# Dilated attention's groups in the order of dilations 4, 16, 1, and a new order of work on ScalarE and VectorE

## The chip, the core and the metric

One NeuronCore of a Trainium2 chip runs the whole program. The metric is device time in microseconds of one execution, the median of several runs. The engines are TensorE (matmuls), VectorE, ScalarE, GpSimd and SyncE; each works through its own queue in order and waits on semaphores for the others.

## What is computed

Two transformer blocks follow each other, on 1024 tokens of width 1024. The first has a convolution layer and a layer of dilated attention, the second has neighbourhood attention, retention and an MLP. The change touches dilated attention alone:

```python
DILATION_GROUPS = ((128, 1), (512, 4), (2048, 16))   # (window, dilation)

def dilated_attention_branch(h, cos, sin, w_in, q_norm, k_norm, w_out):
    q, k, v, gate = jnp.split(h @ w_in, ...)          # 3 groups x 8 heads x 64, gate 512
    q = partial_rope(rms_norm(q, q_norm), cos, sin)
    k = partial_rope(rms_norm(k, k_norm), cos, sin)
    for g, (window, dilation) in enumerate(DILATION_GROUPS):
        o, lse = dilated_band_attention(q[:, :, g], k[:, :, g], v[:, :, g], dilation, window // dilation)
    wts = softmax(stack(lses), axis=0)                # over the three groups
    o = sum(wts[..., None] * stack(outs), axis=0)
    return (o * silu(gate)) @ w_out
```

Each group splits the tokens by residue modulo the dilation; within a residue a query sees itself and up to 128 earlier keys of its own residue. The three outputs of a head are weighted by a softmax over the groups' log denominators.

## The kernel before

Activations stay in SBUF with features on partitions. A matmul with weights ("linear") multiplies a 1024x128 weight tile with all 1024 tokens, in three steps of split precision (high part with high part, high with low, low with high) and two halves of 512 columns: 8 k-tiles of 6 matmuls, 48 in all, into one of two PSUM buffers A and B. SyncE loads weight tiles in pairs in the order of their use, GpSimd splits each into a high and a low part (w_hi, w_lo).

Attention works on four pairs of heads. A pair has ten linears: q, k and v of three groups and the gate. `pair` runs three times in a loop and once more with `last`. Its order is written out by hand on each engine:

- **A group** (`dilated`) has 8 units of 128 queries. In unit u TensorE does the six matmuls of one k-tile of some linear (`products`, L516), the scores of unit u (L723), the product with V of unit u-2 (`values`, L699) and the transposes of the probabilities of unit u-1 (`turn`, L613). VectorE masks the scores and takes the negated maximum (L1745), ScalarE takes the exponential and its sum (`probabilities`, L1202) and later copies the turned probabilities to SBUF as pt (`copy_turned`, L1212), and VectorE takes out the output (`take_out`, L1757). The scores of unit u+1 wait for VectorE's pass over unit u, the product with V for ScalarE's copy.
- A unit has one or two key blocks of 128 (`attn_keys`): dilation 1 has two in each unit but the first, dilation 4 in every other one, dilation 16 one. Units with two have twice the columns in every step.
- The products with V of units 6 and 7 stand inside the next linear, at k = 3 and k = 5 (`rest`).
- **Between groups**, q and k of the next group are prepared: VectorE evacuates the linear (L1591), ScalarE squares it and applies the gain (`square_and_gain`, L1171, L1172), four DMAs issued by ScalarE exchange the rotary halves (`swap_parts`, L1180), VectorE rotates (`rope`, L1774 to L1777), TensorE sums the squares of each head (L536), ScalarE makes inverse roots of them (`roots`), and VectorE applies them while it sorts the tokens by residue (`normalise`, L1783, L1785; `values_in` for v, L1812). For dilation 1 no sorting is needed.
- In dilations 4 and 16 a unit's rows are not the tokens in their order, so the maxima and sums of these groups (`st_own`) go to DRAM by DMA and come back in the tokens' order (`load_stats`, L1241, into `st_x`). Dilation 1 writes `st_x` directly.
- **The shares**: VectorE takes the least of the three negated maxima (`shifts`, L1819), ScalarE exponentiates, VectorE divides (`shares`), ScalarE widens each share to 64 columns (`widen`, L1249), TensorE turns it (`turn_share`, L613), and VectorE multiplies it into the group's output O (`weigh`, L1838). The widened tiles use the buffers wide0, q_sq and vT.
- **The last pair** has no linear under its third group. Behind it come the shares of this pair, the rounding of the four y tiles into high and low parts (`round_ys` on ScalarE, L1307; `split_ys` on VectorE, L1900), and the output projection, whose first two parts cover the first three tiles and then wait for the fourth.

## Time and profile before

| | us |
|---|---|
| median of 3 runs | 2728.7 (2721.8 to 2732.0) |
| profiled execution, its own time | 2727.0 |
| its span in the trace | 2725.2 |
| TensorE busy | 2535.5 (93%) |
| the attention stage | about 640 to 1330 |
| one linear inside it, from 913.3 to 924.3 | 11.0 |

The profile shows one execution. "Busy" counts instructions on an engine, "idle before" the time in front of one with what ended it, PEclk is the clock granted to TensorE as a share of full speed. Lines L... are lines of the kernel.

### The profile page before, as it was taken

To read this page: it belongs to the slowest core of one execution; us is meant where nothing else is said; L and a number is where in the kernel's file an instruction comes from. 1 tells how busy PE (TensorE), PEld (TensorE's weight loads), DVE (VectorE), ACT (ScalarE), POOL (GpSimd) and SP (SyncE) were. 2 spreads that over 40 slices of the span, in tenths; PEclk is the share of its full clock that TensorE was granted. 3 is DMA by queue.
4 is the path that set the end of the run, shared out by engine and by line. 5 is a ranking of instruction groups with operands and counts; after the bars stand their busy time and mean duration, and the time that the engine had idled before them with its cause. 6 is when DMAs were issued, how large, how long until landed. Compare 5 with 4: busy or idle time off the path is not lost.

```text
span 2725.2 us, 31511 instructions
## 1 busy us (share of the span) xinstructions
PE 2535.5 (93%) x11924; PEld 1961.4 (72%) x11924; DVE 1239.4 (45%) x1673; ACT 847.0 (31%) x1263; POOL 866.2 (32%) x437
## 2 busy tenths in 40 slices
PE   7999669999999999898799999999999999999996
PEld 5877348676666666676577677787788888888884
DVE  6999853444544443554644555544421121111223
ACT  5555442324444443444332323322221010010111
POOL 2888743221221221312122222222233333333332
PEclk9999879999999999998899999999999999999998
DMA  3111202111111111111011211221111111111111
GB/s 122 47 46 46 85 11 70 39 53 39 36 36 35 36 28 39 37 36 36 21 59 44 52 41 42 72 66 35 39 46 47 54 47 47 48 53 46 46 46 69
DMA packets 70876, 129.48 MB, mean 48 GB/s; under 512 B 37880, under 2 KB 40952, under 8 KB 70776
## 3 DMA queue, kind: packets, MB, share of 16 engines
q1 hardware_dynamic: 30096, 107.27, 12.5%
q10 hardware_dynamic: 40680, 20.76, 3.4%
q8 instruction: 76, 1.25, 0.2%
q14 instruction: 24, 0.20, 0.0%
HBM read 117.39 MB, written 4.33 MB: 45 GB/s over the span
## 4 chain that ended last, share of the span: by engine, by line
PE 70%; DVE 12%; issue 6%; ACT 5%; ACTq 2%; DMA 2%; POOL 1%; DVEq 0%; SPq 0%; POOLq 0%
PE ps_A L516 31%; PE ps_B L516 26%; PE ps_B L590 2%; PE ps_C L613 2%; PE ps_D L613 2%; POOL ta L451 1%; PE ps_B L723 1%; ACTq L1180 1%; PE ps_C L699 1%; DVE ssum L1564 1%; PE ps_D L699 1%; DMA qT<-q_in 1%; PE ps_A L723 1%; DVE ps_C L1610 1%; DVE kT L1785 1%
## 5 line engine op out<-in xcount | busy, mean ns | idle before, releaser
L433 POOL CAST w_hi<-w_raw 128x1024 fp32r<-128x1024 f32 x162 | 180.3, 1113 | 1686.2 <-issue 805.3
L426 POOL TENSOR_TENSOR w_lo<-w_raw,w_hi 128x1024 fp32r<-128x1024 f32 x188 | 472.0, 2510 | 61.0 <-ACT w_hi L1025 48.0
L516 PE MATMUL ps_A<-HA_hi,w_hi 128*128 128x512 f32 x960 | 313.8, 408 | 48.3 <-POOL HA_lo L475 22.6
L516 PE MATMUL ps_A<-HA_lo,w_hi 128*128 128x512 f32 x960 | 299.3, 393 | 0.0
L516 PE MATMUL ps_A<-HA_hi,w_lo 128*128 128x512 f32 x960 | 299.1, 393 | 0.0
L516 PE MATMUL ps_B<-HA_hi,w_hi 128*128 128x512 f32 x832 | 267.2, 403 | 3.5 <-DVE G L1591 3.3
L516 PE MATMUL ps_B<-HA_lo,w_hi 128*128 128x512 f32 x832 | 258.5, 392 | 0.0
L516 PE MATMUL ps_B<-HA_hi,w_lo 128*128 128x512 f32 x832 | 257.3, 390 | 0.0
L516 PEld LDWEIGHTS ps_A<-HA_hi,w_hi 128*128 128x128 f32 x960 | 176.0, 190 | 97.7 <-issue 47.3
L516 PEld LDWEIGHTS ps_A<-HA_lo,w_hi 128*128 128x128 f32 x960 | 182.2, 190 | 39.2
L516 PEld LDWEIGHTS ps_A<-HA_hi,w_lo 128*128 128x128 f32 x960 | 182.1, 190 | 39.2
L516 PE MATMUL ps_A<-HB_hi,w_hi 128*128 128x512 f32 x640 | 204.0, 400 | 6.8 <-DVE HB_lo L2031 4.2
L1505 ACT ACTIVATE sq<-ta 128x1024 f32<-128x1024 f32 x32 | 34.0, 1062 | 529.7 <-DVE ta L2163 529.7
L516 PE MATMUL ps_A<-HB_lo,w_hi 128*128 128x512 f32 x640 | 198.3, 391 | 0.0
L516 PE MATMUL ps_A<-HB_hi,w_lo 128*128 128x512 f32 x640 | 198.0, 391 | 0.0
L516 PEld LDWEIGHTS ps_B<-HA_lo,w_hi 128*128 128x128 f32 x832 | 157.6, 189 | 33.7
L516 PEld LDWEIGHTS ps_B<-HA_hi,w_lo 128*128 128x128 f32 x832 | 157.0, 189 | 33.6
L516 PEld LDWEIGHTS ps_B<-HA_hi,w_hi 128*128 128x128 f32 x832 | 153.2, 190 | 37.7 <-issue 8.7
L516 PE MATMUL ps_B<-HB_hi,w_hi 128*128 128x512 f32 x512 | 161.1, 396 | 0.0
L516 PE MATMUL ps_B<-HB_lo,w_hi 128*128 128x512 f32 x512 | 157.8, 389 | 0.0
L516 PE MATMUL ps_B<-HB_hi,w_lo 128*128 128x512 f32 x512 | 157.6, 389 | 0.0
L516 PEld LDWEIGHTS ps_A<-HB_hi,w_hi 128*128 128x128 f32 x640 | 118.6, 189 | 35.1 <-issue 8.0
(335 smaller groups left out, 3805.4 us busy)
## 6 DMA issues: line engine op xcount, KB each, us to landing
w_raw<-w_dram SPq DMA_DIRECT2D x188, 512.0 KB, 3.5
X<-x_dram SPq DMA_DIRECT2D x8, 512.0 KB, 8.6
X<-x_dram ACTq DMA_DIRECT2D x8, 512.0 KB, 7.2
out_dram<-X SPq DMA_DIRECT2D x8, 512.0 KB, 2.8
wp_sb<-wp_dram ACTq DMA_DIRECT2D x16, 128.0 KB, 2.0
qT<-q_in ACTq DMA_DIRECT2D x48, 32.0 KB
kT<-k_in ACTq DMA_DIRECT2D x48, 32.0 KB
p_A<-p_dram ACTq DMA_DIRECT2D x2, 512.0 KB, 4.2
```

The source lines that it names most:

```text
L426: pool.tensor_tensor(w_lo[q][:, :, :], w_raw[q][:, :, :], w_hi[q][:, :, :].bitcast(F32), ALU.subtract).then_inc(S[f"w_ready{q}"], 1)
L433: pool.tensor_copy(w_hi[q][:, :, :], w_raw[q][:, :, :]).then_inc(S["w_rounded"], 1)
L451: pool.tensor_tensor(accp[u][:, :], (tap_out[0] if j == 0 else accp[u])[:, :], tap_out[(j + 1) % 2][:, :], ALU.add).then_inc(S["pool_tap"], 1)
L516: op = pe.matmul(AB[b][:, cols], wt[:, w0 + k, :], act[:, k, cols], start=(first and k == ks[0] and step == 0), stop=(last and k == ks[-1] ...
L590: op = pe.matmul(AB[b][:, cols], wp_sb[t][:, k, :], p_sb[k][:, cols], start=(k == 0), stop=(k == PLE_K - 1))
L613: op = pe.transpose(CD[b][:, c * P:(c + 1) * P], src(c), ident[:, :])
L699: op = pe.matmul(CD[slots[u]][d, T - P:T], V[:, k0 + c, d], pt[u % 2][:, (h * nk + c) * P:(h * nk + c + 1) * P], start=(c == 0), stop=(c = ...
L723: op = pe.matmul(AB[other][:, at:at + nk * P], qT[rows, u * P:(u + 1) * P], kT[rows, k0 * P:(k0 + nk) * P], start=True, stop=True)
L1180: act.dma_start(dst[at + d:at + d + ROT_HALF, :], src[at + e:at + e + ROT_HALF, :]) \
L1505: act.activation(sq[:, :], ta[:, :], ACT.Square).then_inc(S["u_sq"], 1)
L1564: dve.tensor_tensor(ssum[:, :], ssum[:, :], sq[:, :], ALU.add).then_inc(S["ssum_added"], 1)
L1610: op = dve.scalar_tensor_tensor(out, win, tap, acc, ALU.mult, ALU.add)
```

## The change

The groups run in the order of dilations 4, 16, 1 (indices 1, 2, 0); the weight tiles are loaded in the matching order. Both exchanges of statistics are then issued before the third group, and the third group needs none. Besides:

- ScalarE's Square of the next q moves from behind unit 1 to behind unit 3, its gain to behind unit 5. The swap of q is issued before k's Square and before the copy of unit 7, the swap of k behind that copy.
- VectorE rotates q before it takes out unit 7 and rotates k before `values_in`.
- TensorE turns the second share at k = 4 and the third at k = 6 of the linear (before: at k = 0 and k = 4). In the last pair it turns two shares before the output projection's first part and the third behind it.
- In the last pair the rounding of the first three y tiles moves into the third group (units 2, 4, 6), and VectorE makes their low parts behind `shares`.

```diff
 N_VEC = _at
+ORDER = (1, 2, 0)
+QKV = [3 * g + k for g in ORDER for k in range(3)] + [9]
+
+
 NA_BLOCKS = [(cb, half) for cb in range(4) for half in range(2)]
 NA_BAND = (0, 8, 24, 32)
 NA_SORT = (2, 1, 1, 0)
...
             sp.dma_start(head_ones[:, :], mats[2]).then_inc(S["head_ones_loaded"], 16)
             sp.dma_start(perm[:, :], mats[3]).then_inc(S["perm_loaded"], 16)
-            with n.loop(sp, ATTN_AT // 2 + 1, w_ready0=1, w_ready1=1) as i:
+            with n.loop(sp, ATTN_AT // 2 - 1, w_ready0=1, w_ready1=1) as i:
                 weight_pair(i * 2 + 2, i * 2 + 3)
+            weight_pair(ATTN_AT + QKV[0], ATTN_AT + QKV[1])
+            weight_pair(ATTN_AT + QKV[2], ATTN_AT + QKV[3])
             with n.loop(sp, PAIRS - 1, w_ready0=5, w_ready1=5) as j:
                 t = j * 10 + ATTN_AT
                 for a, b in ((4, 5), (6, 7), (8, 10), (9, 11), (12, 13)):
-                    weight_pair(t + a, t + b)
-            at = ATTN_AT + 10 * (PAIRS - 1) + 4
+                    weight_pair(*(t + c // 10 * 10 + QKV[c % 10] for c in (a, b)))
+            at = ATTN_AT + 10 * (PAIRS - 1)
+            for c in (4, 6, 8):
+                weight_pair(at + QKV[c], at + QKV[c + 1])
+            at += 10
             with n.loop(sp, (RET_AT - at) // 2, w_ready0=1, w_ready1=1) as i:
                 weight_pair(i * 2 + at, i * 2 + at + 1)
...
                 def shares(k):
                     if k == 0:
                         turn_share(0)
+                    if k == 4:
                         turn_share(1)
-                    if k == 4:
+                    if k == 6:
                         turn_share(0)
-                rest = dilated(0, 0)
+                rest = dilated(ORDER[0], 0)
                 linear(1, HA, pre=sums_at(6, rest))
                 linear(0, HA)
-                rest = dilated(1, 1)
+                rest = dilated(ORDER[1], 1)
                 linear(0, HA, pre=sums_at(6, rest))
                 linear(1, HA)
                 if last:
-                    rest = dilated(2, None)
+                    rest = dilated(ORDER[2], None)
                     rest(3)
                     rest(5)
                     return
-                rest = dilated(2, 0)
+                rest = dilated(ORDER[2], 0)
                 linear(1, HA, pre=rest)
                 linear(0, HA, pre=sums_at(4))
                 linear(1, HA, pre=shares)
...
             pe.wait_ge(S["w_ready0"], n.next("w_ready0"))
             b0 = take_ab()
+            turn_share(0)
+            turn_share(1)
             out_part(b0, 0, 0, range(PAIRS - 1))
-            for i in range(GROUPS):
-                turn_share(i)
+            turn_share(2)
             b1 = take_ab()
             out_part(b1, 0, 1, range(PAIRS - 1))
             out_part(b0, 0, 0, [PAIRS - 1]).then_inc(S["half_done"], 1)
...
                 act.activation(cosT[:, :], turn_of[:, :], ACT.Sin, scale=0.5).then_inc(S["half_sin"], 1)
                 act.activation(sinT[:, :], turn_of[:, :], ACT.Sin).then_inc(S["sin_ready"], 1)
-            def square_and_gain(name, src, sq_of):
-
-                after_ab()
+            def square(name, src, sq_of):
+
                 act.activation(sq_of[:, :], src[:, :], ACT.Square).then_inc(S[name + "_sq"], 1)
+
+            def gain(name, src):
+
                 act.activation(src[:, :], src[:, :], ACT.Identity, scale=col(name + "_gain")) \
                     .then_inc(S[name + "_gained"], 1)
+
+            def square_and_gain(name, src, sq_of):
+
+                after_ab()
+                square(name, src, sq_of)
+                gain(name, src)
             def swap_parts(name, src, dst):
...
                     act.wait_ge(S[f"cd_free{b}"], n.now(f"cd_free{b}"))
                     act.activation(root[:, :], root[:, :], ACT.Exp, scale=-0.5).then_inc(S[name + "_root_ready"], 1)
-            def dilated(g, queries):
+            def dilated(g, queries, between=lambda u: None):
                 def probabilities(u):
                     nk = attn_keys(g, u)[1]
...
                 b, free = next_cd()
                 act.copy(V[:, :, :].rearrange("p b d -> p (b d)"), CD[b][:, :]).then_inc(free, 1)
                 probabilities(1)
-                if queries:
-                    square_and_gain("q", q_in, q_sq)
                 for u in range(2, BLOCKS):
                     copy_turned(u - 2)
                     probabilities(u)
+                    if queries and u == 3:
+                        after_ab()
+                        square("q", q_in, q_sq)
+                    if queries and u == 5:
+                        gain("q", q_in)
+                    between(u)
                 copy_turned(6)
                 def rest():
-                    copy_turned(7)
                     after("unit_done")
                     after("unit_done")
                     act.wait_ge(S["probs_ready"], n.next("probs_ready", BLOCKS))
...
                         for src, dst in stats_moves(st_own[:, g - 1], g, g):
                             act.dma_start(dst, src).then_inc(S["stats_stored"], 16)
                             n.next("stats_stored", 16)
-                return rest
+                return copy_turned, rest
             def load_stats(g):
...
                 settle()
                 act.activation(y_at[:, j, :], y_at[:, j, :], ACT.Silu).then_inc(S["gate_silu"], 1)
+            def round_ys(k):
+                act.copy(YS[0][:, k, :], y_at[:, k, :]).then_inc(S["ys_hi"], 1)
+
+            def early_ys(u):
+
+                if u == 2:
+                    act.wait_ge(S["y_done"], PAIRS - 1)
+                if u in (2, 4, 6):
+                    round_ys(u // 2 - 1)
+
             def pair(j, last):
                 for g in range(2):
-                    rest = dilated(g, True)
+                    copy_turned, rest = dilated(ORDER[g], True)
+                    swap_parts("q", q_in, qT)
                     square_and_gain("k", k_in, k_sq)
+                    copy_turned(7)
+                    swap_parts("k", k_in, kT)
                     rest()
-                    swap_parts("q", q_in, qT)
-                    swap_parts("k", k_in, kT)
                     roots()
                     if g == 1:
-                        load_stats(1)
+                        load_stats(ORDER[0])
+                        load_stats(ORDER[1])
                     pass_ab()
                 if last:
                     after_ab()
                     silu_gate(j)
-                rest = dilated(2, not last)
+                copy_turned, rest = dilated(ORDER[2], not last, early_ys if last else lambda u: None)
+                if not last:
+                    swap_parts("q", q_in, qT)
+                copy_turned(7)
                 rest()
-                load_stats(2)
                 if last:
                     return
                 pass_ab()
-                swap_parts("q", q_in, qT)
                 exp_shares()
                 square_and_gain("k", k_in, k_sq)
                 swap_parts("k", k_in, kT)
...
                 pair(j, last=False)
             pair(PAIRS - 1, last=True)
-            def round_ys(k):
-                act.copy(YS[0][:, k, :], y_at[:, k, :]).then_inc(S["ys_hi"], 1)
-
-            act.wait_ge(S["y_done"], PAIRS - 1)
-            for k in range(PAIRS - 1):
-                round_ys(k)
             exp_shares()
             after("shared_ready")
             for g in range(GROUPS):
...
                         take_out(u - 2)
                 def rest():
-                    take_out(6)
-                    take_out(7)
                     after("turned", 2)
-                return rest
+                return take_out, rest
             def rope(name, src, dst):
...
             def pair(j, last):
                 for g in range(2):
-                    rest = dilated(g)
+                    take_out, rest = dilated(ORDER[g])
                     evacuate(k_in[:, :], g)
+                    take_out(6)
+                    rope("q", q_in, qT)
+                    take_out(7)
                     rest()
-                    rope("q", q_in, qT)
-                    values_in(g ^ 1, g + 1)
                     rope("k", k_in, kT)
-                    normalise(g + 1)
+                    values_in(g ^ 1, ORDER[g + 1])
+                    normalise(ORDER[g + 1])
                     if last and g == 1:
                         evacuate(y_at[:, j, :], 1)
                     else:
                         evacuate(q_in[:, :], g)
-                rest = dilated(2, not last)
+                take_out, rest = dilated(ORDER[2], not last)
                 if not last:
                     evacuate(y_at[:, j, :], 0)
+                take_out(6)
+                if not last:
+                    rope("q", q_in, qT)
+                take_out(7)
                 rest()
                 if last:
                     return
                 shifts()
                 evacuate(k_in[:, :], 1)
                 shares()
-                rope("q", q_in, qT)
                 rope("k", k_in, kT)
-                values_in(0, 0)
-                normalise(0)
+                values_in(0, ORDER[0])
+                normalise(ORDER[0])
                 for g in range(GROUPS):
                     weigh(g)
                 evacuate(q_in[:, :], 1)
...
             rotary_tables()
             rope("q", q_in, qT)
             rope("k", k_in, kT)
-            values_in(0, 0)
-            normalise(0)
+            values_in(0, ORDER[0])
+            normalise(ORDER[0])
             evacuate(q_in[:, :], 1)
             with n.loop(dve, PAIRS - 1, ab_free0=5, ab_free1=5, cd_free0=18, cd_free1=18, lin_done0=5, lin_done1=5,
                         q_swapped=192, k_swapped=192, q_root_ready=3, k_root_ready=3, dve_step=27, scores_done=24,
...
                 dve.tensor_tensor(YS[1][:, k, :], y_at[:, k, :], YS[0][:, k, :].bitcast(F32),
                                   ALU.subtract).then_inc(S["ys_ready"], 1)
+            shifts()
+            shares()
             for k in range(PAIRS - 1):
                 split_ys(k)
-            shifts()
-            shares()
             for g in range(GROUPS):
                 weigh(g)
             gated(PAIRS - 1)
```

## Rows read from the trace of the kernel before

**Rows 1.** The page, part 1: busy time of each engine

```profile
PE 2535.5 (93%) x11924; PEld 1961.4 (72%) x11924; DVE 1239.4 (45%) x1673; ACT 847.0 (31%) x1263; POOL 866.2 (32%) x437
```

**Rows 2.** Waits of TensorE, 640 to 1330 us: total, times, longest

```profile
PE ps_C L699 <- ACT pt L1212: 14.2, 9, 2.0
PE ps_A L516 <- DVE YS_lo L1900: 10.7, 2, 7.2
PE ps_D L613 <- ACT q_sq L1249: 9.8, 3, 3.3
PE ps_D L699 <- ACT pt L1212: 9.2, 5, 2.2
PE ps_B L723 <- DVE q_in L1591: 6.4, 3, 3.0
...
PE ps_A L723 <- DVE q_in L1591: 2.0, 4, 0.6
PE ps_A L723 <- DVE kT L1785: 1.9, 1, 1.9
```

**Rows 3.** Timeline, units of dilation 1: start, us, instruction

```profile
834.71 0.66 PE L699 MATMUL ps_D<-pt,V 128*64 128x128 f32 x8
...
836.82 0.56 ACT L1212 COPY pt<-ps_C 128x512 f32<-128x512 f32 x1
...
837.89 0.66 PE L699 MATMUL ps_C<-pt,V 128*64 128x128 f32 x8
```

**Rows 4.** Timeline, third unit of dilation 1

```profile
822.97 1.04 ACT L1171 ACTIVATE q_sq<-q_in 128x1024 f32<-128x1024 f32 x1
...
823.92 1.13 ACT L1172 ACTIVATE q_in<-q_in,vec 128x1024 f32<-128x1024 f32 x1
...
825.36 0.44 PE L699 MATMUL ps_C<-pt,V 128*64 128x128 f32 x4 [2.01 <-ACT pt L1212]
```

**Rows 5.** Timeline, units of dilation 4 (892), then of dilation 16

```profile
892.02 0.35 ACT L1212 COPY pt<-ps_D 128x256 f32<-128x256 f32 x1
...
892.68 0.44 PE L699 MATMUL ps_D<-pt,V 128*64 128x128 f32 x4
...
939.65 0.44 PE L699 MATMUL ps_C<-pt,V 128*64 128x128 f32 x4
...
941.28 0.35 ACT L1212 COPY pt<-ps_D 128x256 f32<-128x256 f32 x1
...
942.19 0.44 PE L699 MATMUL ps_D<-pt,V 128*64 128x128 f32 x4
```

**Rows 6.** A wait for a share; windows (seventh column PEclk) without and after a stall

```profile
801.55 0.69 PE L613 MATMUL ps_D<-ident,q_sq 128*128 128x128 f32 x2 [3.27 <-ACT q_sq L1249]
...
806.00:807.00 1.00, 1.00 (x6) 0.84 (x5) 0.96 (x2) 0.12 (x1) 0.00 (x0) 1.00 0.00 0
...
882.00:883.00 1.00, 1.00 (x4) 0.81 (x3) 0.00 (x0) 0.00 (x0) 0.00 (x0) 0.50 0.00 0
```

**Rows 7.** Timeline, swap of q and the rotation that waits for it

```profile
851.27 2.65 ACTq L1180 DMA_DIRECT2D qT<-q_in  x4
...
855.65 1.23 DVE L1774 TENSOR_TENSOR q_in<-q_in,cosT 128x1024 f32<-128x1024 f32 x1 [4.21 <-DMA qT<-q_in]
```

**Rows 8.** The last pair's third group: window, and a product with V

```profile
1288.00:1298.00 10.00, 10.00 (x51) 5.44 (x50) 4.42 (x26) 5.49 (x24) 0.00 (x0) 0.50 0.01 2
...
1288.86 0.69 PE L699 MATMUL ps_D<-pt,V 128*64 128x128 f32 x4
```

**Rows 9.** Last product with V, first matmul on the last rounded tile

```profile
1300.47 0.69 PE L699 MATMUL ps_D<-pt,V 128*64 128x128 f32 x4 [0.46 <-ACT pt L1212]
...
1325.88 0.73 PE L516 MATMUL ps_A<-YS_hi,w_hi 128*128 128x512 f32 x2 [3.43 <-DVE YS_lo L1900]
```

**Rows 10.** Timeline, statistics first used, share widened

```profile
1310.42 0.21 DVE L1819 TENSOR_REDUCE least<-st_x 128x16 f32<-128x48 f32 x1
...
1312.20 1.04 ACT L1249 COPY wide<-shared 128x1024 f32<-128x1024 f32 x1 [1.05 <-DVE shared L1830]
```

6 lines of the change are left out of this document (3 added, 3 removed).

## Prediction

> **What bounds the kernel now.** I read the page's engine shares first: TensorE is busy 93% of the span [rows 1], so time is only won where TensorE stands still or works at its lower clock. The change touches the attention stage alone, some 690 us from 640 to 1330 us, so the second view is TensorE's waits in that window [rows 2]. They sum to about 58 us, of four kinds: for ScalarE's copy of turned probabilities (pt), 14.2 + 9.2 us; for ScalarE's widened share, 9.8 us; for VectorE's evacuation of q_in (6.4 + 2.0 us) or its kT (1.9 us); and for the rounded y at the end (10.7 us). The timeline then says what each waits behind. Last, the granted clock: an ordinary microsecond shows 1.00 and six matmul records; one after a stall shows 0.50 and four [rows 6]. Those are the levels 2.4 and 1.2 GHz, so a stall costs more than its own length when the clock falls after it.
>
> **A. The square and gain of q leave the third unit.** In all 11 groups that load a next q, ScalarE runs Square and then gain (L1171, L1172) ahead of the first copy of probabilities, and TensorE waits 2.01 us [rows 4]. The Square takes 0.95 us from start to start; the gain is the rest, 1.04 us. The two pt rows of [rows 2] hold 23.4 us; 1.6 us belong to the last, bare group, so this edit is about 21.8 us. The operations are not removed but moved behind units 3 and 5, one at a time, where they delay the copy that the next unit needs. The slack there is the start of the product with V minus the end of the copy: dilation 1, 837.89 - 837.38 = 0.51 us [rows 3]; dilation 4, 892.68 - 892.37 = 0.31 us; dilation 16, 942.19 - 941.63 = 0.56 us [rows 5]. So each group keeps stalls of (0.95 - slack) + (1.04 - slack): 1.0, 1.4 and 0.9 us. Times 3, 4 and 4 groups that is 12.2 us; dilation 4's copy is still a little late in the third unit, 4 x 0.2, so 13 us stay and 8.8 us go. In three of the four dilation 4 groups the stall also pulled the clock to 0.50 for about 3 us [rows 6]; half of the work of those 3 us is lost, 1.5 us each, 4.5 us. Stalls of 0.7 us should not do that (the group that begins at 640 us stalled 2.0 us without a fall). **A = 13.3 us.** Bounds: no slack at all keeps 22 us and gives 4 us; full slack gives 26.
>
> **B. The second and third share are turned later.** TensorE turned two shares at k = 0 and waited 3.27 us for the second [rows 6], in each of three pairs: 9.8 us. Now it works through four k first, some 5.5 us, so the wait goes. Two of the three stalls were followed by half clock, again some 1.5 us each. VectorE weighs each output behind its turn; its chain gets the strided forms of dilation 4 at this place and ends about when the linear does, so I give it nothing and bound it with 1 us each. **B = 12.8 us** (9 to 14.5).
>
> **C. The chain between two groups.** The swap of q was issued behind the last copy and store, and VectorE idled for it [rows 7]; then it rotated q, took v, rotated k, normalised both and evacuated q_in, and TensorE's scores waited for that. Now the swap of q goes out before copy 7 and the rotation runs before the last output is taken; the swap of k follows, and its rotation runs ahead of values_in. Six operations of 1.23 us [rows 7], 7.4 us, leave the stretch before the scores, which is more than each single wait (0.5 to 3.0 us). What remains is that q_in can only be evacuated after its linear. Of 6.4 + 2.0 + 1.9 us [rows 2] I leave 0.05 us in each of 8 places. **C = 9.9 us** (6 to 10.3). ScalarE's four swap issues hold its queue 2.65 us [rows 7], now ahead of k's Square, k's gain and copy 7. Counted on from the end of copy 6 at 843.7 us, copy 7 ends at 849.2; TensorE asks for it at 850.5. Hidden with 1.3 us to spare.
>
> **D. The last pair.** Its third group runs with no linear under it. It was dilation 16 and becomes dilation 1. Under a linear the two differ by 3.18 - 2.54 = 0.64 us a unit at full clock [rows 3, 5]; the first units are alike, so the covered part wins 7 x 0.64 = 4.5 us. Bare, dilation 16 took (1300.47 - 1288.86) / 6 = 1.94 us a unit at clock 0.50 with TensorE's records full [rows 8]; dilation 1 adds twice 0.64: 3.22 us, and 7 units cost 9.0 us. The three roundings now inside this group (1.04 us each) push ScalarE past its slack by 0.2 us each: 0.6 us. The tail: from the last product with V to the last rounded tile was 1325.88 - 1300.47 = 25.4 us [rows 9], in it 9.2 us from the store at 1301.25 to the first use of the statistics at 1310.42 [rows 10], which goes. But TensorE now turns two shares before its 18 hidden matmuls, and the third turn stands behind these. New tail: last product and copy 1.7; statistics to widened share 1.8 [rows 10]; widen 1.1; two turns at half clock 3.3; 18 matmuls 5.0 (1.5 us of it at half clock); third turn 0.8; weigh and add 2.5, gate 1.2, round 1.1, low part 1.2; handovers 0.4. Sum 20.1 us: 5.3 us won. **D = 4.5 - 9.0 - 0.6 + 5.3 = +0.2 us.**
>
> The Trainium skill, TensorE: Matmul & The Clock Gate (Part 4: PE-mode transpose), says that transposes do not count as TensorE activity the way matmuls do. By that rule the two turns that now lead the tail would not help to raise the clock and the 18 matmuls behind them would run slow throughout, 6.6 us instead of 5.0, a loss of 1.6 us that moves no chance here; the rows of before hold no turns alone after an idle stretch in the tail, so they cannot say.
>
> The exchange of statistics itself, the change's namesake, is worth nothing in the first three pairs: VectorE waited for it, but no wait of TensorE hangs on it [rows 2]. The order of the weight tiles, their number and size stay as they were: zero.
>
> **Sum.** 13.3 + 12.8 + 9.9 + 0.2 = 36.2 us, against the profiled execution's 2727.0 us (span 2725.2): 2690.8 us. The median of before lies 1.7 us above that execution, so I forecast 2692 us, 1.3% faster. A measurement of this kernel tells about 0.5%, 13.6 us, from no change.
>
> **The rivals.**
> 1. *The stall of A is only moved.* If the moved Square and gain find no slack, because units run faster once the first stall is gone, A gives 4 us: 2702 us. For it: the slacks of 0.3 to 0.6 us are smaller than either operation. Against: the units after the stall already run at their steady length [rows 3]. Chance 0.16.
> 2. *The clock stays up in the bare group.* Dilation 1 gives TensorE twice the columns. At 1.00 its own work there is 1.6 us and the round through VectorE and ScalarE about 2 us, so 7 units cost 1 us less than now instead of 9 more, 2684 us with an allowance for the idle start. Against: 0.50 in all ten microseconds from 1288 [rows 8]. Chance 0.12.
> 3. *It does not do what it says.* The waits reappear one step on (A gives 4, B 5, C 3, D 0): 12 us, 2716 us, within 0.5%. For it: in-order queues on four engines often return a wait. Against: each freed wait has another engine's idle time behind it. Chance 0.07.
> 4. *Slower.* VectorE now rotates q before it takes output 7, and that frees the PSUM bank in which TensorE sums k's squares. If the swap lands late, TensorE stands at those sums. From [rows 7] a swap lands 4.4 us after its issue starts: 848.1, rotation to 851.8, output taken by 852.3; the bank is wanted at 854.3, 2 us to spare. The place occurs 8 times; to cost the 36 us won and 14 more, the output must be taken 6.3 us beyond that margin each time, over 8 us late. That gives 2742 us. Chance 0.04, for no swap in before landed so late.
>
> **Numbers.** My forecast has 0.61. The range must hold rivals 1 and 2, the bounds of A (4 to 26), B, C and D (-5 to +9): gains of 17 to 53 us, 2676 to 2712. Faster by over 0.5%: 0.61 + 0.16 + 0.12 = 0.89; within 0.5%: 0.07; slower 0.04.
>
> **What would show it.** The wait for pt at the third unit near zero, and two waits of 0.4 to 0.7 us at the fifth and seventh in each group with a linear (A). No wait for the widened share, and that linear 13.4 us long with its three turns (B). Waits for q_in at the scores under 0.1 us (C). About 3.2 us a unit at clock 0.50 in the bare group, and 20 us from the last product with V to the last rounded tile (D). I am wrong if the fifth and seventh units stall by 1 us or more, if the bare group keeps its clock, or if TensorE starts to wait at the head sums.

## The result

The changed kernel takes 2685.6 us (median of 4, 2685.5 to 2687.4) where the kernel before takes 2728.3 (2721.8 to 2732.0): a ratio of 0.9847, 95% interval 0.9828 to 0.9867. That is inside the range and 6 us below the forecast of 2692. The profiled execution's span is 2683.8 us, 41.4 less than before. First the page, then TensorE's waits in the same stage (total, times, longest); they answer to [rows 1] and [rows 2]:

```profile
PE 2525.6 (94%) x11924; PEld 1953.8 (73%) x11924; DVE 1249.2 (47%) x1673; ACT 849.0 (32%) x1263; POOL 852.5 (32%) x437
```

```profile
PE ps_C L708 <- ACT pt L1231: 9.1, 17, 0.8
PE ps_D L708 <- ACT pt L1231: 6.3, 12, 1.5
PE ps_B L732 <- DVE st_own L1774: 3.6, 3, 1.4
PE ps_C L622 <- ACT wide L1271: 3.4, 1, 3.4
PE ps_C L622 <- ACT sc L1221: 2.9, 4, 2.2
PE ps_A L525 <- DVE YS_lo L1932: 2.2, 1, 2.2
...
PE ps_A L732 <- DVE q_in L1620: 0.5, 1, 0.5
PE ps_B L732 <- DVE q_in L1620: 0.5, 1, 0.5
```

The reader should see four things. The waits for pt fell from 23.4 to 15.4 us, but in 29 pieces instead of 14. The waits for the share q_sq in three pairs are gone; behind the last pair's third group one of 3.4 us for `wide` and one of 2.2 us for the rounded y stand where 10.7 us stood for the rounded y. The waits for q_in and kT at the scores are nearly gone, 1.0 us of 10.3. And there is a wait that hardly was there before (0.2 us): the scores for VectorE's masking pass (st_own), 3.6 us in 3 pieces.

To place gains, all kernels below are measured by **the stage**: from the first scores of the first group to the first matmul on the last rounded tile. In the changed kernel those are these two rows of the timeline:

```profile
642.72 0.49 PE L732 MATMUL ps_B<-kT,qT 64*128 64x128 f32 x4
...
1291.90 0.73 PE L525 MATMUL ps_A<-YS_hi,w_hi 128*128 128x512 f32 x2 [2.21 <-DVE YS_lo L1932]
```

So its stage is 1291.90 - 642.72 = 649.2 us; before it was 1325.88 [rows 9] - 641.22 = 684.7 us. The stage won 35.5 us, the forecast's sum was 36.2. The other 5.9 us of the 41.4 lie in code that is the same in both kernels (below).

From the rows of the scores, one stretch after the other (us). A group is from its first scores to its eighth, a gap from there to the next group's first. A group is covered when TensorE has a linear under it. The bare group, the last pair's third, has none and is taken from its first scores to its last product with V; the tail runs from there to the end of the stage:

| | before | changed |
|---|---|---|
| pair 1, 2, 3: three groups with their gaps | 176.2, 177.5, 177.5 | 167.1, 168.9, 168.5 |
| group of dilation 1, covered | 23.0 | 22.2 |
| group of dilation 4, covered | 21.8 in pair 1, then 23.2 to 23.4 | 21.3 in pair 1, then 22.8, 22.6, 21.9 |
| group of dilation 16, covered | 19.5 | 18.7 |
| the three gaps of a pair, summed | 111.9, 111.6, 111.6 | 105.0, 105.1, 105.0 |
| last pair: two covered groups and gaps | 108.0 | 99.0 |
| last pair: bare group | 20.0 | 26.0 |
| last pair: tail | 25.4 | 19.8 |

### The profile page after: what moved, and what is told of

Its sections match the earlier page's. It is cut to its first block, busy times and chain, and to the rows that moved or that the text cites. A ratio compares the mean times of both kernels' runs of the same rounds, so it can differ in the third digit from the quotient of the medians.

```text
span 2683.8 us, 31485 instructions
## 1 busy us (share of the span) xinstructions
PE 2525.6 (94%) x11924; PEld 1953.8 (73%) x11924; DVE 1249.2 (47%) x1673; ACT 849.0 (32%) x1263; POOL 852.5 (32%) x437
## 4 chain that ended last, share of the span: by engine, by line
PE 74%; DVE 10%; issue 6%; ACT 5%; POOL 2%; ACTq 1%; DVEq 0%; DMA 0%; SPq 0%; POOLq 0%
PE ps_A L525 34%; PE ps_B L525 27%; PE ps_B L599 2%; POOL ta L460 2%; PE ps_C L622 1%; PE ps_D L622 1%; PE ps_C L545 1%; PE ps_D L545 1%; PE ps_B L732 1%; ACT sc L1221 1%; DVE ssum L1593 1%; DVE ps_C L1639 1%; PE ps_B L545 1%; DVE sc L1774 1%; PE ps_C L708 1%
## 5 line engine op out<-in xcount | busy, mean ns | idle before, releaser
L442 POOL CAST w_hi<-w_raw 128x1024 fp32r<-128x1024 f32 x162 | 171.3, 1058 | 1657.8 <-PE ps_A L525 794.5
L525 PE MATMUL ps_A<-HA_hi,w_hi 128*128 128x512 f32 x960 | 314.7, 409 | 46.7 <-POOL HA_lo L484 21.1
```

The lines of the kernel that those rows point to most:

```text
L442: pool.tensor_copy(w_hi[q][:, :, :], w_raw[q][:, :, :]).then_inc(S["w_rounded"], 1)
L525: op = pe.matmul(AB[b][:, cols], wt[:, w0 + k, :], act[:, k, cols], start=(first and k == ks[0] and step == 0), stop=(last and k == ks[-1] ...
```

## The experiments

Stage and rest of the span come from each kernel's own profile; the ratio is to the kernel before on the same chip. The changed kernel's stage came out the same in two profiles, the kernel before's 3.9 us apart, and the others have one profile each. So a difference of under 4 us in the stage (e2, e4, e7) is no proof by itself; what is said of these rests on the waits and gaps in their traces.

| kernel | median | ratio, 95% interval | stage | rest |
|---|---|---|---|---|
| changed | 2685.6 | 0.9847 (0.9828 to 0.9867) | 649.2 | 2034.6 |
| e1 Square back | 2709.1 | 0.9907 (0.9885 to 0.9929) | 667.4 | 2039.9 |
| e2 shares back | 2686.2 | 0.9831 (0.9811 to 0.9851) | 648.3 | 2030.4 |
| e3 chain back | 2692.4 | 0.9859 (0.9835 to 0.9883) | 655.5 | 2034.0 |
| e4 order back | 2690.2 | 0.9837 (0.9816 to 0.9859) | 651.8 | 2036.7 |
| e5 order and shares back | 2708.4 | 0.9922 (0.9895 to 0.9948) | 669.0 | 2038.0 |
| e6 halves | 2680.4 | 0.9815 (0.9790 to 0.9841) | 641.8 | 2037.7 |
| e7 SiLU late | 2686.6 | 0.9835 (0.9808 to 0.9862) | 647.0 | 2040.9 |
| e8 q normalised first | 2682.4 | 0.9826 (0.9800 to 0.9851) | 643.1 | 2031.9 |
| f9 before again | 2725.2 | 0.9994 (0.9976 to 1.0012) | 688.6 | 2032.8 |
| f10 Square alone | 2711.3 | 0.9941 (0.9919 to 0.9962) | 674.7 | 2039.8 |
| f11 changed again | 2687.8 | 0.9852 (0.9832 to 0.9872) | 649.2 | 2038.5 |
| f12 three additions | 2672.1 | 0.9804 (0.9784 to 0.9823) | 635.4 | 2043.3 |

### e1: Square and gain back behind unit 1

```diff
                 probabilities(1)
+                if queries:
+                    square_and_gain("q", q_in, q_sq)
                 for u in range(2, BLOCKS):
...
-                    if queries and u == 3:
-                        after_ab()
-                        square("q", q_in, q_sq)
-                    if queries and u == 5:
-                        gain("q", q_in)
```

> The changed kernel with q's Square and gain back behind unit 1. Measure: the stage, from the first scores of the first group to the first matmul on the last rounded tile (before 684.7 us, changed 649.2 us). Theory: the changed kernel still waits 10.9 us for pt in its 11 covered groups where the kernel before waited 21.8 us, and three of those stalls let the clock fall, so the stage grows by 11 to 15 us, with waits of about 2 us in each third unit and none in the fifth and seventh. Rival (the stall is only moved): under 5 us. Second rival (the clock is what counts): the stage grows by 4 us in the groups where the clock falls and nowhere else.

Measured: the stage grew by 18.2 us, more than the 11 to 15 expected. The waits for pt came back as single ones of 1.6 to 2.2 us at each third unit. The surplus is the clock: it fell behind seven of these eleven waits and not behind four, where the changed kernel has no fall under its covered groups. Dilation 1 lost it in all three pairs, and its group takes 24.6 us (23.0 in the first profile of the kernel before). That this comes from its new place is not shown: in the second profile of the kernel before (f9) dilation 1 lost it too, as the first group. The windows of that stall in pair 1 (seventh column: the granted clock):

```profile
749.00:751.00 2.00, 1.08 (x6) 0.32 (x5) 0.68 (x3) 2.00 (x6) 0.00 (x0) 1.00 0.14 57
751.00:753.00 2.00, 0.91 (x6) 0.61 (x7) 0.39 (x3) 2.00 (x6) 0.00 (x0) 0.81 0.00 0
753.00:756.00 3.00, 3.00 (x11) 2.17 (x10) 0.00 (x0) 0.62 (x2) 0.00 (x0) 0.55 0.00 0
```

Both rivals fell: 18.2 is far from 5, and groups that kept the clock grew too (dilation 16 in the first three pairs from 18.7 to 19.6).

### e2, e4, e5: the places of the shares and the order of the groups

```diff
                 def shares(k):            # e2, e5
                     if k == 0:
                         turn_share(0)
-                    if k == 4:
                         turn_share(1)
-                    if k == 6:
+                    if k == 4:
                         turn_share(0)
```

```diff
-ORDER = (1, 2, 0)                         # e4, e5
+ORDER = (0, 1, 2)
...
                     if g == 1:
-                        load_stats(ORDER[0])
-                        load_stats(ORDER[1])
+                        load_stats(1)
...
                 rest()
+                load_stats(2)
                 if last:
                     return
```

> The changed kernel with the second share turned at k = 0 and the third at k = 4 again. Theory: three waits of 3.3 us and some slow clock come back (12.8 us), but the changed kernel pays some 4 us in new waits at the start of each following pair (scores for VectorE, in the first two units), because VectorE's chain of weighing now ends as late as the linear; these go when the linear is longer. The stage grows by 9 us. Rival (VectorE's chain is the bound there now): the pair's length stays within 1 us of the changed kernel's, stage +3 us or less. Rival (the waits at the start of a pair have another cause): +12 us or more and the new waits stay.

> The changed kernel with the groups in the old order 1, 4, 16, the exchange of dilation 16 behind the third group again, all other edits kept. Theory: the order is worth little. In the first three pairs the waits at the start of a pair (4 us in all) go, and the exchange costs TensorE nothing; in the last pair the bare group gets 6 us shorter, the covered ones 4.5 us longer, the tail 6 to 9 us longer by the exchange. Sum: stage +1 to +4 us. Rival (the exchange was the real cost): stage +15 us or more, with waits of TensorE for a widened share in every pair.

> The changed kernel with both the old order of groups and the old places of the turned shares. Alone, the shares' old places cost the changed kernel's stage -0.9 us, the old order +2.6 us. Theory (two edits remove the same wait): in the new order the exchange is over before the third group, so ScalarE has the second share widened when TensorE asks; in the old order the exchange makes it late and only the later turn hides that. Then both undone together bring the 3.3 us wait back in three pairs, with some half clock behind it: gap from the third group to the next pair 47 to 48 us instead of 43.6 (old order alone) and 46.4 (old places alone), stage 660 to 665 us. Rival (the swap of q and the earlier rotation removed the wait, whatever the order): no wait for a widened share in the first three pairs, gap under 46 us, stage 652 to 655 us.

Measured: e2's stage is 648.3 us, 0.9 *less* than the changed kernel's. I had expected 9 us more; the first rival is nearer in its number. No wait for the second share came back. ScalarE has it widened before TensorE asks for it, as these rows of e2 show (widened from 790.84 to 791.87, turned at 792.06):

```profile
790.84 1.03 ACT L1270 COPY q_sq<-shared 128x1024 f32<-128x1024 f32 x1
...
791.19 1.04 PE L622 MATMUL ps_C<-ident,wide 128*128 128x128 f32 x8
...
792.06 1.04 PE L622 MATMUL ps_D<-ident,q_sq 128*128 128x128 f32 x8
```

e4's stage is 651.8, 2.6 more than the changed kernel's and inside the 1 to 4 expected; it has no wait for q_sq in the pairs either. Its parts: the three pairs 3.4 us less, the last pair's covered part 3.4 more, the bare group 4.2 less, the tail 6.6 more, by one wait of 10.3 us for `wide` where the changed kernel has 3.4. Only both together bring the wait for q_sq back. In e5 the gap behind the third group is 48.5, 49.7 and 48.4 us (e4: 43.6, 43.6, 43.2; e2: 46.4), the stage 669.0 us, and TensorE's waits begin with

```profile
PE ps_C L622 <- ACT wide L1270: 11.1, 1, 11.1
PE ps_D L622 <- ACT q_sq L1270: 10.2, 3, 3.4
```

The theory of e5 holds in its kind and was too low by 4 us: the new order of groups and the later turns each remove the same three waits of 3.3 us, and whichever comes second is worth little. Given the old places of the turns, the new order is worth 669.0 - 648.3 = 20.7 us; given the new ones, 651.8 - 649.2 = 2.6 us. Of the 20.7, the three pairs have 11, the last pair 10: its covered groups 4.4 us (102.3 against 97.9), its tail 8.6 (27.4 against 18.8), and the bare group gives 3.1 back (22.1 against 25.2).

The later turns also cost something in the new order. At 1.6 us less gap per pair (44.8 against 46.4) the first group of the next pair takes 1.5 us longer (22.8 against 21.3). The timeline of the changed kernel at the start of pair 2, and the same place in e2:

```profile
808.50 1.22 DVE L1620 TENSOR_TENSOR q_in<-ps_B,rstd 128x1024 f32<-128x1024 f32 x1
...
809.45 2.37 POOL L435 TENSOR_TENSOR w_lo<-w_raw,w_hi 128x1024 fp32r<-128x1024 f32 x1
809.64 3.26 DVE L1873 TENSOR_TENSOR y_at<-O,y_at 128x1024 f32 x1
...
809.87 0.49 PE L732 MATMUL ps_B<-kT,qT 64*128 64x128 f32 x4
...
814.18 0.70 PE L732 MATMUL ps_B<-kT,qT 64*128 64x256 f32 x4 [1.41 <-DVE st_own L1774]
```

```profile
807.00 1.23 DVE L1619 TENSOR_TENSOR q_in<-ps_B,rstd 128x1024 f32<-128x1024 f32 x1 [1.70 <-PE ps_B L525]
...
808.14 1.22 DVE L1872 TENSOR_TENSOR y_at<-O,y_at 128x1024 f32 x1
808.17 3.43 POOL L435 TENSOR_TENSOR w_lo<-w_raw,w_hi 128x1024 fp32r<-128x1024 f32 x1
...
811.21 0.70 PE L732 MATMUL ps_B<-kT,qT 64*128 64x256 f32 x4
```

VectorE's product for y (L1873) takes 3.26 us when GpSimd's subtraction started 0.2 us before it, and 1.22 us when it starts first; then GpSimd's takes 3.43 instead of 2.37. In the changed kernel VectorE's chain (v, q, k, five weighing operations, q_in) runs without a pause up to this product, so it falls just behind GpSimd's start. The masking pass for the first scores stands behind it, and TensorE waits 1.41 us for that. The Trainium skill, GPSIMD Engine Reference (Specifications), lists the SBUF interfaces as shared with VectorE where that has two SBUF inputs; these rows agree. They also show who pays: the one that starts second. It is the same at the start of pairs 3 and 4, where VectorE's product starts 0.20 and 0.19 us behind GpSimd's and takes 3.26 and 3.24 us; in e2 it starts 0.03 us ahead in all three places and takes 1.22.

### e3: swap and rotation back

```diff
                     copy_turned, rest = dilated(ORDER[g], True)
-                    swap_parts("q", q_in, qT)
                     square_and_gain("k", k_in, k_sq)
                     copy_turned(7)
-                    swap_parts("k", k_in, kT)
                     rest()
+                    swap_parts("q", q_in, qT)
+                    swap_parts("k", k_in, kT)
                     roots()
...
                     take_out(6)
-                    rope("q", q_in, qT)
                     take_out(7)
                     rest()
-                    rope("k", k_in, kT)
+                    rope("q", q_in, qT)
                     values_in(g ^ 1, ORDER[g + 1])
+                    rope("k", k_in, kT)
```

> The changed kernel with the swap of q behind copy 7 and the store, and VectorE's old order (outputs, rotate q, values, rotate k), between the first two pairs of groups of each head pair; the third group's end keeps its new order. Theory: waits of 0.5 us before the second group and 1.7 to 3.0 us before the third come back, 8 in all, stage +10 us; dilation 4 now stands first and its store (1.3 us on ScalarE) precedes the swap in both places, so the first of them may be 1 us longer each: +10 to +14 us. Rival (the earlier swap gained nothing, since VectorE had time): under 4 us.

Measured: stage +6.3 us, between theory (10 to 14) and rival (under 4). The gaps tell why. Before the second group all four grew, by 3.2, 1.8, 1.9 and 1.1 us. Before the third group none did: 29.8, 29.8, 29.8, 27.9 us with and without the edit. There the next group is now dilation 1, whose v, q and k need no sorting, and VectorE is in time either way. So the 2.5 to 3.9 us that this gap lost against before have two causes that overlap: the new order alone gives all of it (e3), and the earlier swap in the old order most of it (e4 has 30.8, 30.8, 30.7 and 28.9 where before had 32.4, 32.3, 33.7 and 30.9). The stage grew by less than the 8.0 us of the gaps because bare group and tail came out 1.6 us shorter in this execution.

### f10: Square and gain moved, nothing else

```diff
...
                 probabilities(1)
-                if queries:
-                    square_and_gain("q", q_in, q_sq)
                 for u in range(2, BLOCKS):
                     copy_turned(u - 2)
                     probabilities(u)
+                    if queries and u == 3:
+                        after_ab()
+                        square("q", q_in, q_sq)
+                    if queries and u == 5:
+                        gain("q", q_in)
```

> The kernel before with one edit: q's Square behind unit 3, its gain behind unit 5. Theory: the groups get 8 to 13 us shorter in sum, but the third group's chain is unchanged, so the waits for q_in and for the widened share stay; stage 672 to 677 us. Rival (in-order queues return it: units that end earlier meet VectorE's chain, which does not): the waits for q_in grow by what the units gain, stage 680 us or more.

Measured: stage 674.7 us, 10.0 less than the first profile of before and 13.9 less than its second (f9); the waits for q_in (5.2 + 2.0 us, before 6.4 + 2.0) and for q_sq (9.9 us) are those of before. The rival falls: no wait for q_in grew. The gaps sum to 398.4 us against 396.9 before; the 1.3 us more in pair 1 stand where the clock was at 0.50 for 6.8 us around the share's wait, in before for 3.4. Of the whole kernel's time this one edit is worth 0.6%.

### e6, e7, e8, f12: what the waits that remain are worth

e6 puts Square and gain in halves behind the units 2 to 5, e7 moves the last pair's SiLU, e8 fills VectorE's idle time ahead of v, f12 has all three:

```diff
-                    if queries and u == 3:             # e6, f12
-                        after_ab()
-                        square("q", q_in, q_sq)
-                    if queries and u == 5:
-                        gain("q", q_in)
+                    if queries and u in (2, 3):
+                        if u == 2:
+                            after_ab()
+                        half = slice((u - 2) * HALF, (u - 1) * HALF)
+                        op = act.activation(q_sq[:, half], q_in[:, half], ACT.Square)
+                        if u == 3:
+                            op.then_inc(S["q_sq"], 1)
+                    if queries and u in (4, 5):
+                        half = slice((u - 4) * HALF, (u - 3) * HALF)
+                        op = act.activation(q_in[:, half], q_in[:, half], ACT.Identity, scale=col("q_gain"))
+                        if u == 5:
+                            op.then_inc(S["q_gained"], 1)
...
-                if last:                               # e7, f12, ScalarE
-                    after_ab()
-                    silu_gate(j)
...
             for g in range(GROUPS):
                 widen(g, g)
                 next_cd()
+            after_ab()
+            silu_gate(PAIRS - 1)
...
-                values_in(0, ORDER[0])                 # e8, f12, VectorE
-                normalise(ORDER[0])
+                normalise(ORDER[0], lambda: values_in(0, ORDER[0]))    # q, then v, then k
...
+                roots()                                # e8, f12, ScalarE
                 after("shared_ready")
                 widen(0, 0)
-                roots()
...
-                linear(0, HA, pre=sums_at(4))          # e8, f12, TensorE
+                linear(0, HA, pre=sums_at(3))
```

> The changed kernel with Square and gain each in two halves of 512 columns, one half behind each of the units 2 to 5. Theory (each operation is late by its length less the slack of 0.3 to 0.56 us): a half takes some 0.55 us, so dilations 1 and 16 wait 0 to 0.1 us and dilation 4 some 0.25 us a half; of the 11 us of waits for pt in covered groups some 3 to 4 us stay, stage -7 us. Rival (ScalarE's time as a whole is what lacks, so that four operations instead of two cost more by their fixed part): stage 0 to +3 us.

> The changed kernel with the last pair's SiLU of the gate (and its two table loads) moved from ahead of the bare third group to behind the widened shares, where ScalarE waits for VectorE. Theory: TensorE's wait for the first probabilities (2.2 us) falls to 0.3 us or less, and with it the idle time before the clock falls; the bare group takes 24 us instead of 26 by the wait alone, and 20 to 22 us if the clock stays at 1.00. Stage -2 us at least, -6 us at most. Rival (the wait is not ScalarE's table work but VectorE's pass): no change; rival (the tail's gate is now late): tail +2 us.

> The changed kernel with, at the end of a pair, q normalised before v is taken, the roots ahead of the first widened share on ScalarE, and the head sums at k = 3 instead of 4. Theory: VectorE's chain (v, q, k, five weighing operations) ends about with the linear, so the gating of y falls on GpSimd's split and takes 3.3 us instead of 1.2, and TensorE waits 1.4 us at the second scores of the next pair. If the chain ends 2 us earlier, by filling VectorE's idle 1.8 us before v, the gap plus the next group's start shrink by 1.5 to 2.5 us a pair, stage -4 to -7 us. Rival (the gating collides with GpSimd wherever it starts, since both follow the linear's end): the operation still takes over 3 us, stage -1 us or less.

> The changed kernel, unchanged, on the chip of the next one. Stage 649 us within 2 us; waits as before, since they follow from the order of work and not from the chip.

> The changed kernel with the three additions together: Square and gain in halves, SiLU late in the last pair, VectorE's q normalised first. Alone they took 7.4, 2.2 and 6.1 us off the stage. They act on different waits (pt in the units; the first probabilities of the bare group; the gating of y), so the theory has them add up: stage 633 to 636 us, 0.5 to 0.7% faster than the changed kernel on the same chip. Rival (shorter units bring VectorE's chain back onto the path between groups): waits for q_in over 1 us and a stage above 638 us.

Measured: e6 took 7.4 us off the stage (expected 7). Its waits for pt are 7.0 us, of which 5.4 lie in the bare group; in the covered groups 1.6 us are left of 10.9, where I expected 3 to 4. What is left, 0.19 and 0.28 us a group in dilation 4 and none in the others, is again a length less the slack. That 9.3 us of waits bring only 7.4 has one clear cause: in pair 3 the clock fell to 0.50 from 977 to 980 us behind a wait of 1.34 us for VectorE, and that first group took 23.4 us. e7 took 2.2 us off, the lower end: the wait for the first probabilities went from 2.2 to 0.2 us and the bare group from 26.0 to 24.3, the tail did not grow (19.1), but the clock fell all the same, only later:

```profile
1250.00:1254.00 4.00, 2.79 (x18) 1.40 (x18) 1.83 (x10) 3.86 (x11) 0.92 (x1) 1.00 0.38 128
1254.00:1258.00 4.00, 3.22 (x18) 1.91 (x20) 0.91 (x5) 2.33 (x7) 0.00 (x0) 0.62 0.01 5
1258.00:1262.00 4.00, 2.59 (x25) 1.68 (x25) 1.85 (x9) 3.16 (x9) 0.00 (x0) 0.95 0.02 4
```

e8 took 6.1 us off the stage. VectorE's product for y starts ahead of GpSimd's subtraction again, and the second scores come 2.8 us behind the first instead of 4.3:

```profile
807.98 1.21 DVE L1874 TENSOR_TENSOR y_at<-O,y_at 128x1024 f32 x1
808.01 3.44 POOL L435 TENSOR_TENSOR w_lo<-w_raw,w_hi 128x1024 fp32r<-128x1024 f32 x1
...
808.60 0.49 PE L732 MATMUL ps_B<-kT,qT 64*128 64x128 f32 x4
...
811.44 0.70 PE L732 MATMUL ps_B<-kT,qT 64*128 64x256 f32 x4
```

The first groups of pairs 2 and 3 are at 21.3 us, as in pair 1. Of the 6.1 us they and the last pair's (20.8 against 21.9) explain 3.9; bare group and tail 1.4 (the clock stood at 0.50 for 6 us there and not 10), and 0.8 us lie in the gaps. f11 repeats the changed kernel's stage at 649.2 us. f12's is 635.4, 13.8 less: 7.4 + 2.2 + 6.1 = 15.7 were to be had if all added up, and 633 to 636 was expected. The rival falls: no wait for q_in is in its list. Its longest waits:

```profile
PE ps_D L708 <- ACT pt L1231: 4.6, 4, 1.5
PE ps_C L708 <- ACT pt L1231: 3.7, 11, 0.8
PE ps_C L622 <- ACT wide L1278: 3.4, 1, 3.4
```

f12 is the fastest kernel here: 2672.1 us against 2687.8 for the changed kernel in the same five rounds, 0.6% less.

### f9: the kernel before once more

> The kernel before, unchanged, for a second profile. The code ahead of and behind the stage is the same in all kernels here, and its time came out between 2030.4 and 2041.1 us, in steps with the granted clock after short waits. Theory (that spread is the clock's timing and not the change): the stage repeats at 684.7 us within 3 us, the rest falls anywhere in that band. Rival (the kernel before is slow outside the stage too): the rest repeats at 2040 us or more while every kernel with the changed code stays near 2035.

Measured: the rest of the span came to 2032.8 us where the first profile had 2040.5, so the kernel before is not slow there; the rival falls. The stage came to 688.6, 3.9 us more and just outside the 3 I allowed. The waits are the same, but the clock fell in other places. Dilation 4 took 21.6 to 21.8 us in all four pairs, where three had 23.2 to 23.4. Dilation 1 took 24.4 to 24.6 in pairs 2 to 4 instead of 23.0, and dilation 16 took 21.1 to 22.6 instead of 19.5. The same wait of 2.01 us in pair 2 (before at 825.36, f9 at 823.71) has these windows behind it, the first from before and the second from f9:

```profile
826.00:829.00 3.00, 3.00 (x23) 1.96 (x22) 0.50 (x4) 0.89 (x3) 0.00 (x0) 1.00 0.00 0
```

```profile
824.00:827.00 3.00, 3.00 (x13) 2.48 (x10) 0.29 (x1) 1.24 (x5) 0.00 (x0) 0.50 0.00 0
```

So where the clock falls behind a wait of this length is not fixed by the program. Both profiles of the changed kernel have no fall at all between 640 us and its bare group.

## Why the prediction was right

The sum was right to 1 us on the stage, the terms less so, and that close a fit is partly luck: D came out 4.0 us better than its term, and 3.4 us were given back that B had at nothing. The kernel's time of 2685.6 us lies in fact nearer to rival 2's 2684 than to the forecast, but not by rival 2: 5.9 us of it lie outside the stage. Measured terms come from the table of groups and gaps; they add up to 12.7 + 22.6 - 3.4 + 4.2 = 36.1 us, against 35.5 from mark to mark.

**A, 13.3 us forecast, 12.7 measured.** Dilation 1 lost 0.88 us in each of 3 groups, dilation 16 0.84 in each of 4, dilation 4 0.5 in each of 4, and the three falls of the clock are gone (about 1.55 each, from 23.4 against 21.8 us). That there were three is the first profile's; f9 has six groups lengthened by a fall, so this term is the least certain. The two waits per group came out as forecast from the slacks: 0.62 + 0.71 us for dilation 4 (1.4 forecast), 0.42 + 0.52 for dilation 1 (1.0), 0.36 + 0.47 for dilation 16 (0.9), and in the last pair some 0.2 less each. The 0.2 us in dilation 4's third unit came in pair 1 alone. The fifth unit of dilation 4, to be held against [rows 4, 5]:

```profile
822.44 1.04 ACT L1181 ACTIVATE q_sq<-q_in 128x1024 f32<-128x1024 f32 x1
...
823.39 0.35 ACT L1231 COPY pt<-ps_C 128x256 f32<-128x256 f32 x1
...
823.79 0.44 PE L708 MATMUL ps_C<-pt,V 128*64 128x128 f32 x4 [0.62 <-ACT pt L1231]
```

Rival 1, the stall that is only moved, is thus refuted. f10 (10.0 and 13.9 us against the two profiles of before) and e1 (18.2, with seven falls of the clock in it) bound the price from both sides.

**B and C, 22.7 us forecast, 22.6 measured in the gaps, less 3.4 us given back.** The three pairs' gaps fell by 6.9, 6.5 and 6.6 us, the last pair's by 3.2, of which 0.64 belongs to the narrower groups. The step that failed is B's "its chain gets the strided forms of dilation 4 at this place and ends about when the linear does, so I give it nothing": it ends when the linear does, and then meets GpSimd, which costs 1.5, 1.3 and 0.6 us at the start of pairs 2, 3 and 4, against the 21.3 us of pair 1 (in pair 4 it is 1.1 us against e8's 20.8). I had bounded that with 1 us each. The sign for C, waits for q_in under 0.1 us, was missed by two of 0.5 us.

**The exchange.** The step "The exchange of statistics itself ... is worth nothing in the first three pairs" is wrong as put. No wait of TensorE hung on it directly, but the wait for the second share did, two steps further on: exchange, shares, widening. e2 and e5 show it. The number did not suffer because the later turns remove the same wait, and I had booked it there; that, too, is luck.

**D, 0.2 us forecast, 4.2 measured** (4.5 - 5.9 + 5.6). The covered part's 4.5 us stand as forecast here; e5 against e2, the old order against the new with the turns in their old places, gives 4.4 (102.3 against 97.9). The bare group cost 5.9 us more than before instead of 9.6, because the clock came back inside it:

```profile
1254.00:1256.00 2.00, 1.94 (x8) 0.89 (x6) 0.09 (x2) 2.00 (x6) 0.00 (x0) 0.50 0.00 0
1262.00:1266.00 4.00, 3.05 (x28) 1.97 (x28) 2.01 (x10) 2.79 (x8) 0.00 (x0) 1.00 0.00 0
```

Scores follow each other at 3.2 and 3.5 us while it is at 0.50 (3.22 forecast) and at 2.9 and 1.9 us at the end. There the roundings cost more than the 0.2 us forecast: a product waits 1.01 us for its copy behind the second and 1.50 us behind the third, where the last two, with no rounding ahead, wait 0.77 and 0.67.

```profile
1266.65 1.03 ACT L1279 CAST YS_hi<-y_at 128x1024 fp32r<-128x1024 f32 x1
...
1267.58 0.57 ACT L1231 COPY pt<-ps_D 128x512 f32<-128x512 f32 x1
...
1268.21 0.66 PE L708 MATMUL ps_D<-pt,V 128*64 128x128 f32 x8 [1.50 <-ACT pt L1231]
```

So rival 2 was half right: the clock did not stay up, but it came back, as it did in all nine profiles here that have dilation 1 last. The tail took 19.8 us against 20.1 forecast and 25.4 before, and the 18 matmuls in it 5.0 us, from 1279.51 to 1284.55, as forecast. The Trainium skill, TensorE: Matmul & The Clock Gate (Part 4: PE-mode transpose), says that the full clock does not engage for transposes. The measurement differs, and it decides: by that rule the prediction had put these matmuls at 6.6 us. The windows with the two leading turns, which start at 1276.21, and the first matmuls behind them:

```profile
1276.00:1279.50 3.50, 3.29 (x16) 3.32 (x17) 3.42 (x4) 1.85 (x2) 0.00 (x0) 0.50 0.00 0
1279.50:1281.00 1.50, 1.50 (x6) 1.21 (x5) 1.03 (x1) 0.00 (x0) 0.00 (x0) 0.50 0.00 0
1281.00:1282.00 1.00, 1.00 (x5) 0.83 (x4) 0.97 (x2) 0.00 (x0) 0.00 (x0) 0.86 0.00 0
```

The clock is at 1.00 some 5.1 us after the first turn and 1.8 us after the first matmul. In the tail of before, where no turn led, it rose 4.8 us after the first matmul (1308.38 to about 1313.2):

```profile
1311.00:1313.00 2.00, 2.00 (x6) 1.53 (x5) 0.88 (x4) 0.95 (x2) 0.00 (x0) 0.50 0.00 0
1313.00:1314.00 1.00, 1.00 (x5) 0.77 (x5) 0.00 (x0) 1.00 (x2) 0.00 (x0) 0.91 0.00 0
```

A rival remains in these two, for TensorE had stood still for 3.4 us ahead of the turns and for 7.2 us ahead of the matmuls. e5 settles it. There the two turns come behind 11.1 us of standing still, at 1293.18, and the clock is at 1.00 from about 1298.0, 4.8 us behind the first turn and 1.5 us behind the first matmul:

```profile
1297.50:1298.50 1.00, 1.00 (x5) 0.81 (x4) 0.97 (x2) 0.00 (x0) 0.00 (x0) 0.76 0.00 0
```

**What the forecast did not have: 5.9 us outside the stage.** Fourteen profiles of kernels with the same code there gave 2030.4 to 2043.3 us; the kernel before is in it with 2040.5 and 2032.8, the changed one with 2034.6 and 2038.5. The profiles differ in whether the granted clock falls behind short waits. Half of the time at 0.50 outside the stage, from 150 us on, is 38.7 us in e2, the shortest, and 51.1 in f12, the longest; that is nearly all of their 12.9 us. Between the first profiles of before and changed it is 46.1 against 45.0, so most of these 5.9 us stays unexplained. What decides where the clock falls in a given execution stays open too. This spread is about as large as what I took for the kernel's resolution, 0.5%, and it is why the stage was the better measure here.

## What to carry to other kernels

Work moved into a pipelined stretch costs its length less the slack of the operation that it delays, and that slack can be read as the start of the consumer minus the end of the producer; split the work until the pieces fit. Before a wait is credited to one edit, ask which other edit of the same change removes it too: here either the order of groups or the place of two transposes would do. And where an engine that has just been relieved of idle time meets a shared interface, look at who starts first.

## What the runs showed of the hardware

- VectorE and GpSimd on operations with two SBUF inputs: the one that starts second waits for the other. 3.26 us instead of 1.22 for VectorE's when it starts 0.19 us later, 3.43 instead of 2.37 us for GpSimd's when it starts 0.03 us later.
- A stall of 2.0 us can leave the granted clock at 1.00 in one execution and drop it to 0.50 in the next, in the same place of the same kernel: dilation 1's third unit in pair 2 kept it in the first profile of before and lost it in f9. A fall came even behind a stall of 1.34 us (e6).
- With 16 transposes ahead of the matmuls the clock rose 5.1 us (changed) and 4.8 us (e5) behind the first transpose, 1.8 and 1.5 us behind the first matmul; where no transpose led, it rose 4.8 us behind the first matmul (before).
- In the bare group, short matmuls with pauses, the clock stayed at 0.50 to the end once it had fallen in all five profiles with one key block a unit ([rows 8], f9, f10, e4, e5). With two key blocks it regained 1.00 in all nine, and fell again before the end in four of them (e6, e7, f11, f12).
